# One vector operation in place of two in the router and the selection, and each gather of the first group behind the matrix that used to come after it

## The chip, the cores and the metric

The kernel runs on one core of a Trainium2 chip. The metric is the device time of one execution in microseconds (us). The engines meant below are PE (TensorE, the matrix engine), DVE (VectorE), ACT (ScalarE), POOL (GpSimd) and SP (SyncE, which here only issues transfers from main memory).

## What is computed

One layer of an encoder on 256 tokens of width 2048: attention, and behind it a mixture of 32 experts. The change touches only the second half, which in the reference is (cut):

```python
def hierarchical_moe(h, rg_w, rg_b, re_w, re_b, w_gu, w_d):
    g_prob = jax.nn.softmax((hf @ rg_w).astype(f32) + rg_b.astype(f32), axis=-1)
    g_p, g_idx = lax.top_k(g_prob, 1)
    e_logits = ((hf @ re_w).astype(f32) + re_b.astype(f32)).reshape(n_tok, MOE_GROUPS, MOE_EXPERTS_PER_GROUP)
    e_logits = e_logits[jnp.arange(n_tok), g_idx[:, 0]]
    e_p, e_idx = lax.top_k(jax.nn.softmax(e_logits, axis=-1), MOE_TOP_K)
    e_p = e_p / jnp.sum(e_p, axis=-1, keepdims=True)
    weight = g_p * e_p
    expert_id = g_idx * MOE_EXPERTS_PER_GROUP + e_idx
    ...
        g, u = jnp.split(xb @ w_gu[e], 2, axis=-1)
        return (jax.nn.silu(g) * u) @ w_d[e]
```

Each token chooses one of 4 groups and in it 2 of 8 experts. An expert has a matrix `w_gu` of 2048 x 1024 and a matrix `w_d` of 512 x 2048, all in float32, together 12 MB. The 32 experts make 400 MB, which must all be read.

## The kernel before

Attention comes first; its weights and those of the experts go through one **ring** of six slots of 2 MB in the on-chip memory (`ring`). SP issues the loads in a fixed order (`load_item`), one per slot; ahead of each it waits until the semaphore `w_used` says that PE has read what lay in the slot. An expert takes six loads (four quarters of `w_gu`, j = 0 to 3, and two halves of `w_d`, j = 4 and 5). Five of them of the first two experts lie in other tiles that were free early (`SPARE`, `HALF_SPARE`: the tiles `arena`, `ada_ring`, `region_a`, `held`), so they need no slot.

Experts are worked on in **groups of four** (`moe_group`, 8 groups: the first is written out, the next six are a loop on each engine, the last is written out as the tail). Further groups for experts with over 32 tokens are planned by `plan_further_items`; none ran in the profile. In a group:

- DVE makes the selection `sel_w`, 128 tokens x (4 experts x 32 slots) for each of the two token halves (`for a in range(TT)`, TT = 2), as a comparison of a rank table with slot numbers, and from it `sel`, scaled by the norm of the token. With that it raises `sel_ready`.
- PE gathers the tokens of the four experts by matmuls with `sel`, in four parts of the width: `gather(0)` to `gather(3)`, each 8 matmuls of 128 x 128 into a PSUM bank of its own.
- For each part DVE reads the bank, scales and shifts it into `x_items` (two operations of 128 x 512) and raises `items_ready`.
- For each expert i PE multiplies `x_items` by the four quarters of `w_gu`. For i = 0 quarter j needs part j of `x_items`, so it waits for `items_ready`, j + 1. Before the change the gathers run one ahead: gather 0, gather 1, quarter 0, gather 2, quarter 1, gather 3, quarter 2, quarter 3. After each of the quarters `w_used` rises by one.
- While PE does quarter 3 of the first expert, DVE in the first group runs `weigh` (the weights of the chosen experts, small operations) and then scales `sel_w` by them (`selw_ready`); PE transposes that.
- ACT and DVE form `silu(g) * u` (`gate_exp`, `hid_ready`), PE transposes it and multiplies by the two halves of `w_d`.
- After four experts PE adds the results to the tokens (`y_done`, `y_added`), and the next group begins.

In the first group DVE also runs `plan_further_items` behind the third expert's results, over 40 small operations. SP waits for its end (`tables_ready`) before it issues the loads of the second group's first expert.

**Ahead of the first group** stands the router. DVE turns the logits of both token halves into a choice (`first_max` for the group, then `by_group` and `e_log`, the logits of the chosen group; `first_max` twice more for the two experts; `outer`, which spreads the choice over 32 experts into `chosen`). PE ranks the tokens by a few small matmuls, and DVE makes `rank1`, from which the selection is made. Every operation of DVE here waits for the one before it (`step.link`). PE has nothing else to do until `sel_ready`.

Of the kernel before, what the change touches and what calls it, by code (L numbers as in the profile page):

```python
# [17 lines left out]
P = 128  # L18
T = 256
TT = T // P  # L20
# [4 lines left out]
EXPERTS, GROUPS, PER_GROUP = 32, 4, 8  # L25
FF = 512
FT = FF // P
SLOTS = 32
QUAD = 4
# [38 lines left out]
def encoder_layer(nc, x, c, ada_w, ada_b, norm1_g, norm2_g, router_g_w, router_g_b, router_e_w, router_e_b,  # L68
# [3 lines left out]
    ALU, ACT, AX = mybir.AluOpType, mybir.ActivationFunctionType, mybir.AxisListType  # L72
    X = AX.X

    ctx = ExitStack()
    with ctx:
# [25 lines left out]
        slot_no = sb("slot_no", [P, SLOTS])  # L102
# [50 lines left out]
        sel = carve(4096, TT, QUAD, SLOTS)  # L153
        sel_w = carve(4352, TT, QUAD, SLOTS)
# [4 lines left out]
        rank1 = carve(6016, TT, ITEMS)  # L159
        weight = carve(6112, TT, ITEMS)  # L160
        rt = carve(6208, 448)
        logits = rt[:, 0:72].rearrange("p (a n) -> p a n", a=TT)
        by_group = rt[:, 72:136].rearrange("p (a n) -> p a n", a=TT * GROUPS)
# [43 lines left out]
        ssq, rstd = stat[:, 0:2], stat[:, 2:4]  # L207
# [392 lines left out]
        def _(pe):  # L600
# [444 lines left out]
            def moe_group(g, first=False, tail=False):  # L1045
# [78 lines left out]
                for i in range(2 if tail else QUAD):  # L1124
                    m = g * QUAD + i
                    for j in range(4):
# [3 lines left out]
                        if i == 0 and j < 3:  # L1130
                            gather(j + 1)
# [19 lines left out]
                        if j < 3:  # L1151
                            last.then_inc(w_used, 1)
                    last.then_inc(w_used, 1)
# [332 lines left out]
        def _(dve):  # L1486
# [344 lines left out]
            for a in range(TT):  # L1831
                part = by_group[:, GROUPS * a:GROUPS * (a + 1), :]
                step.link(v.tensor_tensor(part, logits[:, a, GROUPS:].rearrange("p (g e) -> p g e", g=GROUPS),
                                          g_hot[:, a, :].unsqueeze(2).to_broadcast([P, GROUPS, PER_GROUP]),
                                          ALU.mult))
                step.link(v.reduce_sum(e_log[:, a, :], part.rearrange("p g e -> p e g"), X))
# [8 lines left out]
            def outer(dst, per_expert):  # L1845
                for a in range(TT):
                    ins = v.tensor_tensor(dst[:, a, :].rearrange("p (g e) -> p g e", g=GROUPS),
                                          g_hot[:, a, :].unsqueeze(2).to_broadcast([P, GROUPS, PER_GROUP]),
                                          per_expert[:, a:a + 1, :].to_broadcast([P, GROUPS, PER_GROUP]), ALU.mult)
                    if a < TT - 1:  # L1850
                        step.link(ins)
                return ins
# [69 lines left out]
            def moe_group(g, tab, first_group=False, tail=False):  # L1922

                wide4 = [P, QUAD, SLOTS]
                for a in range(TT):
                    r = rank1[:, a, bass.ds(tab * QUAD, QUAD)]
                    step.link(v.tensor_tensor(sel_w[:, a, :, :], slot_no[:].unsqueeze(1).to_broadcast(wide4),
                                              r.unsqueeze(2).to_broadcast(wide4), ALU.is_equal))

                for a in range(TT):  # L1930
                    ins = v.tensor_scalar(sel[:, a, :, :], sel_w[:, a, :, :], rstd[:, a:a + 1], None, ALU.mult)  # L1931
                    if a < TT - 1:
                        step.link(ins)
                ins.then_inc(sel_ready, 1)
# [13 lines left out]
                for a in range(TT):  # L1948
                    w = weight[:, a, bass.ds(tab * QUAD, QUAD)]
                    ins = v.tensor_tensor(sel_w[:, a, :, :], sel_w[:, a, :, :], w.unsqueeze(2).to_broadcast(wide4),  # L1950
                                          ALU.mult)
                    if a < TT - 1:
                        step.link(ins)
                ins.then_inc(selw_ready, 1)
# [70 lines left out]
            per_group = TT + (TT - 1) + 4 + (TT - 1) + 3 * QUAD  # L2025
# [51 lines left out]
```

## Time and profile before

| | |
|---|---|
| median of 3 runs | 1489.13 us (1489.03 to 1489.66) |
| profiled execution, its time | 1489.31 us |
| its span in the trace | 1487.5 us |
| PE busy | 1148.3 us, 77% |
| DVE busy | 633.7 us, 43% |
| read from main memory | 575.02 MB, 388 GB/s over the span |

The span is what the trace covers; 1.8 us of the execution's own time lie around it. The shares of busy time are averages over two very different stages: attention and its weights up to some 550 us, and the experts behind it.

### The profile page before, as it was taken

To read this page: it belongs to the slowest core of one execution; us is meant where nothing else is said; L and a number is where in the kernel's file an instruction comes from. 1 tells how busy PE (TensorE), PEld (TensorE's weight loads), DVE (VectorE), ACT (ScalarE), POOL (GpSimd) and SP (SyncE) were. 2 spreads that over 40 slices of the span, in tenths; PEclk is the share of its full clock that TensorE was granted. 3 is DMA by queue.
4 is the path that set the end of the run, shared out by engine and by line. 5 is a ranking of instruction groups with operands and counts; after the bars stand their busy time and mean duration, and the time that the engine had idled before them with its cause. 6 is when DMAs were issued, how large, how long until landed. Compare 5 with 4: busy or idle time off the path is not lost.

```text
span 1487.5 us, 20513 instructions
## 1 busy us (share of the span) xinstructions
PE 1148.3 (77%) x8480; PEld 736.7 (50%) x8480; DVE 633.7 (43%) x1026; ACT 175.3 (12%) x395; POOL 95.7 (6%) x122
## 2 busy tenths in 40 slices
PE   3899999999999998767567667668558558567655
PEld 3788888888888885333133124224214224224222
DVE  4766768777747524452132123124114114214214
ACT  3011242222134120300000000000000000000002
POOL 3211101121100000000000000000000000000001
PEclk9999999999999999979789689789779879879888
DMA  8999999999995477999999999999999999999996
GB/s 316 383 387 388 399 376 383 385 392 381 357 374 195 165 299 304 425 420 404 428 427 429 428 430 428 427 429 429 428 429 428 428 429 428 428 428 429 427 427 244
DMA packets 116139, 577.92 MB, mean 389 GB/s; under 512 B 10250, under 2 KB 51296, under 8 KB 90484
## 3 DMA queue, kind: packets, MB, share of 16 engines
q1 hardware_dynamic: 89572, 474.37, 78.4%
q0 software_dynamic: 26512, 102.77, 17.9%
q8 instruction: 40, 0.66, 0.2%
q14 instruction: 15, 0.12, 0.0%
HBM read 575.02 MB, written 2.10 MB: 388 GB/s over the span
## 4 chain that ended last, share of the span: by engine, by line
PE 53%; DMA 37%; DVE 6%; issue 1%; ACT 1%; SPq 0%; DVEq 0%; ACTq 0%
DMA ring<-in_moe_w_gu_dram 26%; PE psum L770 9%; PE psum L1147 8%; PE psum L734 7%; DMA ring<-in_moe_w_d_dram 7%; PE psum L1054 5%; PE psum L1176 4%; PE psum L744 4%; DMA ring<-in_da_w_in_dram 4%; PE psum L1199 3%; PE psum L965 3%; PE psum L886 2%; PE psum L878 2%; DVE arena L1525 1%; PE psum L681 1%
## 5 line engine op out<-in xcount | busy, mean ns | idle before, releaser
L1147 PE MATMUL psum<-ring,ada_ring 128*32 128x256 f32 x3696 | 276.7, 450 | 143.5 <-DMA ring<-in_moe_w_gu_dram 143.4
L1147 PEld LDWEIGHTS psum<-ring,ada_ring 128*32 128x32 f32 x3696 | 125.0, 121 | 290.3 <-DMA ring<-in_moe_w_gu_dram 190.3
L1176 PE MATMUL psum<-ring,arena 128*32 128x512 f32 x960 | 157.0, 803 | 27.0 <-ACT arena L1444 16.0
L1975 DVE TENSOR_SCALAR arena<-arena 128x128 f32<-128x128 f32 x32 | 7.3, 227 | 348.5 <-ACT arena L1438 348.5
L1992 DVE TENSOR_TENSOR arena<-psum,arena 32x512 f32<-32x512 f32 x108 | 74.1, 686 | 187.5 <-PE psum L1176 177.3
L770 PE MATMUL psum<-region_b,ring 128*128 128x256 f32 x512 | 113.8, 380 | 4.1 <-ACT region_b L1301 2.6
L734 PE MATMUL psum<-region_b,ring 128*128 128x256 f32 x512 | 112.0, 379 | 0.0
L770 PEld LDWEIGHTS psum<-region_b,ring 128*128 128x128 f32 x512 | 96.6, 190 | 18.0 <-ACT region_b L1301 3.3
L734 PEld LDWEIGHTS psum<-region_b,ring 128*128 128x128 f32 x512 | 96.7, 190 | 12.8
L1438 ACT ACTIVATE arena<-psum 128x128 f32<-128x128 f32 x32 | 8.9, 278 | 783.9 <-PE psum L1147 742.2
L1176 PEld LDWEIGHTS psum<-ring,arena 128*32 128x32 f32 x960 | 37.2, 134 | 124.9 <-issue 83.0
L1525 DVE SCALAR_TENSOR_TENSOR arena<-ada_ring,silu_c,arena 128x512 f32<-128x512 f32 x120 | 90.2, 752 | 19.1 <-DMA ada_ring<-in_ada_w_dram 15.4
L1054 PE MATMUL psum<-arena,region_b 128*128 128x128 f32 x512 | 74.8, 311 | 22.6 <-DVE arena L1931 17.5
L1054 PEld LDWEIGHTS psum<-arena,region_b 128*128 128x128 f32 x512 | 70.2, 222 | 35.4 <-issue 34.1
L1545 DVE SCALAR_TENSOR_TENSOR held<-ada_ring,silu_c,held 128x1024 f32<-128x1024 f32 x60 | 77.1, 1284 | 15.2 <-DMA ada_ring<-in_ada_w_dram 13.5
L1545 DVE SCALAR_TENSOR_TENSOR arena<-ada_ring,silu_c,arena 128x1024 f32<-128x1024 f32 x60 | 77.0, 1283 | 9.4 <-DMA ada_ring<-in_ada_w_dram 7.8
L770 PE MATMUL psum<-ring,region_b 128*128 128x256 f32 x256 | 58.7, 386 | 5.5 <-DMA ring<-in_da_w_in_dram 5.5
L594 POOL TENSOR_TENSOR region_b<-region_a,ada_ring 128x1024 f32<-128x1024 f32 x3 | 7.1, 2357 | 864.1 <-DVE region_a L1968 864.1
L1165 PE MATMUL psum<-ident,arena 128*128 128x128 f32 x30 | 10.6, 353 | 66.1 <-DVE arena L1978 66.1
L567 POOL DMA_DIRECT2D ada_ring<-in_ada_w_dram x64 | 45.1, 704 | 234.0 <-DVE held L1545 108.6
L1199 PE MATMUL psum<-arena 128*128 128x512 f32 x112 | 51.6, 615 | 8.7 <-DVE arena L1992 4.8
L744 PE MATMUL psum<-ring,region_b 128*128 128x256 f32 x256 | 55.9, 379 | 0.0
(269 smaller groups left out, 1112.1 us busy)
## 6 DMA issues: line engine op xcount, KB each, us to landing
ring<-in_moe_w_gu_dram SPq DMA_DIRECT2D x123, 2048.0 KB, 25.6
ring<-in_moe_w_d_dram SPq DMA_DIRECT2D x62, 2048.0 KB, 24.4
ada_ring<-in_ada_w_dram POOLq DMA_DIRECT2D x88, 1024.0 KB, 10.9
ring<-in_da_w_in_dram SPq DMA_DIRECT2D x15, 2048.0 KB, 34.7
ring<-in_da_w_in_dram SPq DMA_DIRECT2D x18, 1024.0 KB, 23.8
ring<-in_da_w_out_dram SPq DMA_DIRECT2D x8, 2048.0 KB, 20.6
ada_ring<-in_ada_w_dram POOLq DMA_DIRECT2D x16, 512.0 KB, 12.9
ring<-in_moe_w_d_dram SPq DMA_DIRECT2D x8, 512.0 KB, 19.4
```

The source lines that it names most:

```text
L567: gp.dma_start(ada_ring[:, j % ADA_CH, :].rearrange("p (k n) -> p k n", k=2), w_ada[:, 2 * j:2 * j + 2, bass.ds(n * 2 * ADA_BLK, 2 * ADA_B ...
L734: last = mm(psum[:, B_Q + j, T * i:T * (i + 1)], slot16(s)[:, k, P * i:P * (i + 1)], h_t[:, k, :], start=k == 0, stop=k == KT - 1)
L744: last = mm(psum[:, B_V, VD * a:VD * (a + 1)], h_t[:, k, P * a:P * (a + 1)], slot16(s)[:, k, :], start=k == 0, stop=k == KT - 1)
L770: return mm(psum[:, bank, T * a:T * (a + 1)], lhs, rhs, **flags)
L965: last = mm(psum[:, bank, 0:VD], lhs[:, k, :], w[:, k0 + k, :], start=k == 0 and not more, stop=k == 7, skip_group_check=True)
L1054: last = mm(psum[:, B_G + q, P * kk:P * (kk + 1)], x_res[:, a, P * k:P * (k + 1)], sel[:, a, :, :].rearrange("p a b -> p (a b)"), start=a ...
L1147: last = mm(psum[32 * n:32 * n + 32, B_GU, 0:256].rearrange("p (a b) -> p a b", a=2), x_items[:, k, SLOTS * i:SLOTS * (i + 1)], w[:, :, n ...
L1176: last = mm(psum[32 * n:32 * n + 32, B_D + i % 2, :], hid_t[:, k, :], w[:, kk, n, :], start=k == 0, stop=k == FT - 1)
L1199: mm(psum[:, B_G + n, :], sel_t[:, a, :], o_items[:, 512 * n:512 * (n + 1)], start=True, stop=True).then_inc(y_done, 1)
L1525: ins = v.scalar_tensor_tensor(out=acc_b, in0=w, scalar=silu_c[:, k:k + 1], in1=acc_b, op0=ALU.mult, op1=ALU.add)
L1545: ins = v.scalar_tensor_tensor(out=row, in0=w, scalar=silu_c[:, k:k + 1], in1=row, op0=ALU.mult, op1=ALU.add)
L1992: v.tensor_tensor(o, src, gate2[32 * n:32 * n + 32, cols], ALU.mult).then_inc(o_ready, 1)
```

## The change

Two kinds of edit. First, on DVE, pairs of operations, one for each token half, become single operations over both: the product and the sum that make `e_log`, the two calls of `outer`, and in every group the comparison for `sel_w`, its scaling into `sel` (a tensor_scalar with a column becomes a tensor_tensor with a broadcast column) and its scaling by the weights. Second, on PE, in the first group only, `gather(j + 1)` no longer stands ahead of quarter j of the first expert but behind it.

```diff
-                        if i == 0 and j < 3:
+                        if i == 0 and j < 3 and not first:
                             gather(j + 1)
                         if spare is not None:
                             pe.wait_ge(spare_loaded[spare], 32)
...
                         if j < 3:
                             last.then_inc(w_used, 1)
+                        if first and i == 0 and j < 3:
+                            gather(j + 1)
...
-            for a in range(TT):
-                part = by_group[:, GROUPS * a:GROUPS * (a + 1), :]
-                step.link(v.tensor_tensor(part, logits[:, a, GROUPS:].rearrange("p (g e) -> p g e", g=GROUPS),
-                                          g_hot[:, a, :].unsqueeze(2).to_broadcast([P, GROUPS, PER_GROUP]),
-                                          ALU.mult))
-                step.link(v.reduce_sum(e_log[:, a, :], part.rearrange("p g e -> p e g"), X))
+            both = [P, TT, GROUPS, PER_GROUP]
+            hot_groups = g_hot.unsqueeze(3).to_broadcast(both)
+            step.link(v.tensor_tensor(by_group, logits[:, :, GROUPS:].rearrange("p a (g e) -> p a g e", g=GROUPS),
+                                      hot_groups, ALU.mult))
+            step.link(v.reduce_sum(e_log, by_group.rearrange("p a g e -> p a e g"), X))
...
             def outer(dst, per_expert):
-                for a in range(TT):
-                    ins = v.tensor_tensor(dst[:, a, :].rearrange("p (g e) -> p g e", g=GROUPS),
-                                          g_hot[:, a, :].unsqueeze(2).to_broadcast([P, GROUPS, PER_GROUP]),
-                                          per_expert[:, a:a + 1, :].to_broadcast([P, GROUPS, PER_GROUP]), ALU.mult)
-                    if a < TT - 1:
-                        step.link(ins)
-                return ins
+                return v.tensor_tensor(dst.rearrange("p a (g e) -> p a g e", g=GROUPS), hot_groups,
+                                       per_expert.unsqueeze(2).to_broadcast(both), ALU.mult)
...
-                wide4 = [P, QUAD, SLOTS]
-                for a in range(TT):
-                    r = rank1[:, a, bass.ds(tab * QUAD, QUAD)]
-                    step.link(v.tensor_tensor(sel_w[:, a, :, :], slot_no[:].unsqueeze(1).to_broadcast(wide4),
-                                              r.unsqueeze(2).to_broadcast(wide4), ALU.is_equal))
-
-                for a in range(TT):
-                    ins = v.tensor_scalar(sel[:, a, :, :], sel_w[:, a, :, :], rstd[:, a:a + 1], None, ALU.mult)
-                    if a < TT - 1:
-                        step.link(ins)
-                ins.then_inc(sel_ready, 1)
+                both4 = [P, TT, QUAD, SLOTS]
+                r = rank1[:, :, bass.ds(tab * QUAD, QUAD)]
+                step.link(v.tensor_tensor(sel_w, slot_no[:].unsqueeze(1).unsqueeze(1).to_broadcast(both4),
+                                          r.unsqueeze(3).to_broadcast(both4), ALU.is_equal))
+                v.tensor_tensor(sel, sel_w, rstd.unsqueeze(2).unsqueeze(3).to_broadcast(both4), ALU.mult)\
+                    .then_inc(sel_ready, 1)
```

What stands in a row on PE at the head of the first group, before the change (L1054 is a gather, L1147 a quarter of `w_gu`, L1043 the last matmul of the ranks, L1159 the transposes of `sel_w`; the trace counts each float32 matmul twice, so x8 here is x16 there):

```order
L1043 MATMUL psum<-arena,ones 128x32
L1054 MATMUL psum<-arena,region_b 128x128 x16
L1147 MATMUL psum<-ring,ada_ring 32x256 x16
L1054 MATMUL psum<-arena,region_b 128x128 x8
L1147 MATMUL psum<-ring,ada_ring 32x256 x16
L1054 MATMUL psum<-arena,region_b 128x128 x8
L1147 MATMUL psum<-ring,ada_ring 32x256 x16
L1147 MATMUL psum<-arena,ada_ring 32x256 x8
L1147 MATMUL psum<-ada_ring 32x256 x8
L1159 MATMUL psum<-ident,arena 128x128 x2
```

And after it, at the same place (the transposes are L1161 here):

```order
L1043 MATMUL psum<-arena,ones 128x32
L1054 MATMUL psum<-arena,region_b 128x128 x8
L1147 MATMUL psum<-ring,ada_ring 32x256 x16
L1054 MATMUL psum<-arena,region_b 128x128 x8
L1147 MATMUL psum<-ring,ada_ring 32x256 x16
L1054 MATMUL psum<-arena,region_b 128x128 x8
L1147 MATMUL psum<-ring,ada_ring 32x256 x16
L1054 MATMUL psum<-arena,region_b 128x128 x8
L1147 MATMUL psum<-arena,ada_ring 32x256 x8
L1147 MATMUL psum<-ada_ring 32x256 x8
L1161 MATMUL psum<-ident,arena 128x128 x2
```

The same matmuls stand there; the second gather has moved from ahead of the first quarter to behind it, the third and the fourth likewise by one quarter, so that each quarter now stands directly behind the gather whose result it needs.

On DVE, from the end of the router to the first parts of `x_items`, before the change (L1847 is `outer`, L1856 `rank1`, L1927 the comparison, L1931 the scaling into `sel`, L1940 and L1943 `x_items`):

```order
L1843 TENSOR_TENSOR arena<-arena 128x16
L1847 TENSOR_TENSOR arena<-arena 128x32 x2
L1856 SCALAR_TENSOR_TENSOR arena<-psum,arena 128x2x32
L1927 TENSOR_TENSOR arena<-slot_no,arena 128x128 x2
L1931 TENSOR_SCALAR arena<-arena,stat 128x128 x2
L1940 TENSOR_TENSOR ada_ring<-psum,a 128x512
L1943 TENSOR_TENSOR ada_ring<-ada_ring,mod 128x512
```

And after it (the comparison is L1922, the scaling L1924, `x_items` L1931 and L1934):

```order
L1844 TENSOR_TENSOR arena<-arena 128x16
L1847 TENSOR_TENSOR arena<-arena 128x64
L1852 SCALAR_TENSOR_TENSOR arena<-psum,arena 128x2x32
L1922 TENSOR_TENSOR arena<-slot_no,arena 128x256
L1924 TENSOR_TENSOR arena<-arena,stat 128x256
L1931 TENSOR_TENSOR ada_ring<-psum,a 128x512
L1934 TENSOR_TENSOR ada_ring<-ada_ring,mod 128x512
```

Three pairs of operations have become three operations of twice the size; nothing has changed its place.

## Rows read from the trace of the kernel before

**Rows 1.** Stretches: bounds, length, busy of PE, PEld, DVE, ACT, POOL, clock, DMA, GB/s

```profile
560.00:568.00 8.00, 7.29 (x64) 6.18 (x64) 3.35 (x7) 0.00 (x0) 0.00 (x0) 0.79 0.08 32
...
588.00:670.00 82.00, 59.21 (x547) 27.68 (x543) 41.95 (x89) 15.43 (x15) 7.23 (x2) 0.88 1.00 423
670.00:674.00 4.00, 4.00 (x56) 2.83 (x52) 1.44 (x3) 0.00 (x0) 0.00 (x0) 1.00 0.73 225
674.00:780.00 106.00, 70.27 (x650) 30.23 (x639) 27.06 (x51) 2.61 (x9) 0.00 (x0) 0.84 1.01 427
...
1400.00:1463.00 63.00, 36.98 (x379) 13.63 (x383) 9.38 (x19) 3.15 (x8) 0.00 (x0) 0.81 1.01 422
```

**Rows 2.** Timeline of SP's queue: start us, length, the load issued

```profile
568.19 0.33 SPq L477 DMA_DIRECT2D ring<-in_moe_w_d_dram  x1
...
670.74 0.33 SPq L474 DMA_DIRECT2D ring<-in_moe_w_gu_dram  x1
```

**Rows 3.** Timeline of PE, head of the first group (gathers L1054, quarters L1147)

```profile
560.71 5.47 PE L1054 MATMUL psum<-arena,region_b 128*128 128x128 f32 x32 [1.17 <-DVE arena L1931]
566.10 2.02 PE L1147 MATMUL psum<-ring,ada_ring 128*32 128x256 f32 x32
568.05 2.05 PE L1054 MATMUL psum<-arena,region_b 128*128 128x128 f32 x16
570.03 2.02 PE L1147 MATMUL psum<-ring,ada_ring 128*32 128x256 f32 x32
...
576.71 1.11 PE L1147 MATMUL psum<-ada_ring 128*32 128x256 f32 x16
```

**Rows 4.** Timeline of DVE there: the parts of x_items

```profile
564.43 0.69 DVE L1940 TENSOR_TENSOR ada_ring<-psum,a 128x512 f32<-128x512 f32 x1 [3.78 <-PE psum L1054]
565.16 0.69 DVE L1943 TENSOR_TENSOR ada_ring<-ada_ring,mod 128x512 f32<-128x512 f32 x1
...
570.14 0.69 DVE L1940 TENSOR_TENSOR ada_ring<-psum,a 128x512 f32<-128x512 f32 x1 [2.51 <-PE psum L1054]
```

**Rows 5.** Timeline of DVE, router to selection, and an operation of 256 columns

```profile
548.95 0.42 DVE L1799 TENSOR_TENSOR arena<-psum,ada_ring 128x256 f32<-128x256 f32 x1 [6.25 <-PE psum L878]
...
554.27 0.18 DVE L1833 TENSOR_TENSOR arena<-arena 128x32 f32<-128x32 f32 x1
...
555.20 0.17 DVE L1820 TENSOR_REDUCE arena<-arena 128x2 f32<-128x16 f32 x1
...
557.76 0.42 DVE L1847 TENSOR_TENSOR arena<-arena 128x32 f32<-128x32 f32 x2
...
559.39 0.62 DVE L1927 TENSOR_TENSOR arena<-slot_no,arena 128x128 f32<-128x128 f32 x2
560.04 0.61 DVE L1931 TENSOR_SCALAR arena<-arena,stat 128x128 f32<-128x128 f32 x2
```

**Rows 6.** Timeline at the first expert's end: weigh, selection, gate

```profile
575.40 0.18 DVE L1863 COPY arena<-psum 128x32 f32<-128x32 f32 x1
...
577.90 0.62 DVE L1950 TENSOR_TENSOR arena<-arena 128x128 f32<-128x128 f32 x2
577.91 0.28 ACT L1438 ACTIVATE arena<-psum 128x128 f32<-128x128 f32 x1 [20.02 <-PE psum L1147]
578.43 0.22 DVE L1975 TENSOR_SCALAR arena<-arena 128x128 f32<-128x128 f32 x1
```

**Rows 7.** Timeline from the plan to the second group's first gathers

```profile
637.58 0.23 DVE L1975 TENSOR_SCALAR arena<-arena 128x128 f32<-128x128 f32 x1
...
662.99 5.60 PE L1054 MATMUL psum<-arena,region_b 128*128 128x128 f32 x32 [5.13 <-issue]
```

**Rows 8.** Busy time by stretches, for the clock (columns as in rows 1)

```profile
561.00:564.00 3.00, 3.00 (x16) 3.00 (x16) 0.00 (x0) 0.00 (x0) 0.00 (x0) 0.50 0.00 0
581.50:584.50 3.00, 3.00 (x20) 0.85 (x16) 0.00 (x0) 0.00 (x0) 0.00 (x0) 0.50 1.03 434
594.00:597.00 3.00, 0.70 (x5) 0.29 (x9) 1.76 (x4) 0.70 (x2) 0.00 (x0) 1.00 1.01 415
```

More of the change, by code:

```diff
@@ L162, in encoder_layer @@
         logits = rt[:, 0:72].rearrange("p (a n) -> p a n", a=TT)
-        by_group = rt[:, 72:136].rearrange("p (a n) -> p a n", a=TT * GROUPS)
+        by_group = rt[:, 72:136].rearrange("p (a g n) -> p a g n", a=TT, g=GROUPS)
         chosen = rt[:, 136:200].rearrange("p (a n) -> p a n", a=TT)
@@ L1947, in moe_group @@
                     weigh()
[L1948 to L1954, printed above, removed]
+                w = weight[:, :, bass.ds(tab * QUAD, QUAD)]
+                v.tensor_tensor(sel_w, sel_w, w.unsqueeze(3).to_broadcast(both4), ALU.mult).then_inc(selw_ready, 1)
                 def keep_last(q):
@@ L2024, in _ @@
             moe_group(0, 0, first_group=True)
-            per_group = TT + (TT - 1) + 4 + (TT - 1) + 3 * QUAD
+            per_group = 1 + 4 + 3 * QUAD
             extra_groups = dve.value_load(extra_i[0:1, EXTRA:EXTRA + 1], min_val=0, max_val=EXTRA // QUAD)
```

## The prediction

> **What bounds the kernel now.** I read the stretches first, since the share of busy time is a mean over stages. From 674 us to 1463 us the DMA engines are busy all the time and move 422 to 429 GB/s [rows 1]. In that stretch the experts' matrices come as fast as they can, and PE and DVE wait for them. Nothing that either engine does faster or slower there can move the end; what counts is the moment at which the stream starts to run without a hole. So I looked for holes. There is a large one from 560 to 568 us (share 0.08, 32 GB/s), then a full stretch from 588 to 670 us (423 GB/s), and a last one from 670 to 674 us (share 0.73, 225 GB/s: against 428 GB/s, (1 - 225/428) x 4 = 1.9 us of transfer are missing) [rows 1].
>
> The last hole is the one that dates the stream. It ends with a load that SP issues at 670.74 us [rows 2], as PE has just read the first quarter of the second group's first expert: the gathers began at 662.99 us [rows 7], and the slot was free at 670.7. The ring had run dry a moment before. What comes before 662.99 is a chain without a DMA wait in it: back over the fourth expert of the first group, whose gate DVE took up at 637.58, right at the end of its plan for further groups [rows 7], over the third and the second expert to the first one [rows 6], to the gathers [rows 3], to the selection and the router [rows 5]. So a microsecond more or less in that chain moves the load at 670.74 us by as much, and with it the end. For a longer chain this is exact, since the hole is already there; a shorter one would gain until the hole of about 2 us is closed.
>
> **The gathers.** Before the change PE has no wait from 566.10 us on: quarter, gather, quarter, gather, quarter, quarter, the last ending at 576.71 + 1.11 = 577.82, so 11.72 us [rows 3]. DVE makes a part of `x_items` in two operations, 0.73 us from one start to the next and 0.69 us for the second, 1.42 us in all [rows 4], and all of it lies under the gather or quarter that PE does meanwhile. After the change each quarter stands right behind its own gather, and PE has nothing else to do while DVE works. That cover is gone, and the 1.42 us come in full. One round is then:
>
> - gather, 568.05 to 570.03: 1.98 us [rows 3];
> - from its end to DVE's start, 570.03 to 570.14: 0.11 us [rows 3, 4];
> - DVE: 1.42 us [rows 4];
> - from DVE's end to PE's start, as between the selection (560.04 + 0.61) and the first gather (560.71): 0.06 us [rows 3, 5];
> - quarter, 566.10 to 568.05: 1.95 us [rows 3].
>
> That makes 5.52 us. From the start of quarter 0 to the end of quarter 3 it takes 1.95 + 3 x 5.52, and 0.07 for the end of the last quarter (2.02 long instead of its step of 1.95): 18.58 us. Against 11.72 that is **+6.86 us**. The second gather, which now stands inside, is in that figure; ahead of quarter 0 it leaves almost nothing, because quarter 0 had to wait for `x_items` anyway: these were ready at 565.16 + 0.69 = 565.85 [rows 4], with the 0.06 above 565.91, and it began at 566.10. **-0.19 us**. This is all that the new order saves ahead of the first freed slot. The second slot comes 5.52 us after the first and no longer 568.05 to 572.0, 3.9 us; the third later still.
>
> **DVE ahead of the gathers.** Every operation waits for the one before, and PE waits for the last. The four small operations for `e_log` take 554.27 to 555.20, 0.93 us, about 0.23 each [rows 5]. What a wider one costs I take from 128 columns at about 0.31 against 256 at 0.42 us [rows 5]: 0.11 for 128 columns, so 0.03 for 32 more. Two operations of 0.26 make 0.52: -0.41. `outer`: 0.42 for two, one of 0.20 + 0.03: -0.19. Comparison and scaling: from 559.39 to 560.65, 1.26 us for four [rows 5]; two of 0.42 with a gap of 0.04: 0.88, -0.38. The scaling becomes a tensor_tensor with two broadcast inner dimensions, a form the trace does not show. Its bounds are one half's 0.31 below and two halves' 0.62 above; I take 0.42, since the comparison (a tensor_tensor with broadcast) and the scaling cost the same for 128 columns, 0.62 and 0.61 for two [rows 5]. For all five edits the same bounds give 0 to about 1.3 us of saving; I take the sum, **-0.98 us**.
>
> **The weights and the gate of the first expert.** `weigh` and the scaling of `sel_w` run from 575.40 to the gate's first operation at 578.43, 3.03 us [rows 6]. They lose 0.19 (`outer`) and 0.20 (0.62 to 0.42). Counted from 575.40, quarter 3 used to end at +2.42 and the gate came 0.61 behind it. Now `x_items`, whose last operation ends 0.08 behind that point, starts quarter 3 after 0.06, and it ends at +0.08 + 0.06 + 2.02 = +2.16; DVE would reach the gate at 3.03 - 0.39 = +2.64, 0.48 behind it. ACT would let it at 0.42 (0.09 to its start, 0.28, 0.05), so DVE stays last. **-0.13 us**.
>
> **Every other group.** The selection's saving of some 0.4 us lies where the stream is full. In the second group, the one ahead of the last hole, PE's idle time ahead of the gathers is ended by "issue", its own way into the loop, not by DVE [rows 7]. 0 us for all of them, and nothing moves in the tail.
>
> **The sum** is 6.86 - 0.19 - 0.98 - 0.13 = +5.56 us. Against the profiled execution's own 1489.31 us (span 1487.5) this gives 1494.9; that execution is 0.2 us above the median, so I forecast **1494.7 us**. Cover elsewhere? The loads for the third and fourth expert are issued as slots come free, the first that matters behind the first expert, so they are late by the same 5.5 us, and so is the plan behind which the fourth expert waits.
>
> **The clock.** PE's granted clock was at 0.50 (1.2 GHz) from 561 to 564 us, just as the first gathers ran, and again from 581.5 to 584.5; ahead of the first, DVE had let PE wait 1.17 us for the selection [rows 3, 8]. At 594 to 597 it had 0.70 us of work in 3 us and the clock stayed at 1.00 [rows 8]. Each such stretch costs 3 x (1 - 0.5) = 1.5 us when matmuls fill it. After the change PE is busy 3.93 of 5.52 us in each round, far more than in these pauses. So I count no new fall and leave the two old ones where they are. If both happened to miss the work, the end would come at 1494.7 - 3.0 = 1491.7; falls do not keep still from run to run, so this is the low side of my range, and a larger price of DVE's wider forms the other way adds up to 1.0.
>
> **Rivals.**
>
> *The clock falls between the rounds.* Three pauses of 1.59 us now stand where PE had none. For it: two of the idle spells in this stage were followed by half clock. Against it: a spell with a quarter of the work was not [rows 8]. One fall costs 1.5 us, two 3.0: 1496.2 or 1497.7 us. The Trainium skill, "TensorE: Matmul & The Clock Gate", section "A second HAM failure mode: psum-queue depth-cycling", speaks for this rival: short idle moments between groups of matmuls, as the engine goes from PSUM bank to bank, are enough to make the clock swing between its two levels. By that rule the time would be that of two falls, by the rows on the pauses that of none.
>
> *The first hole dates the stream, and the change gains.* Then the load at 568.19 us [rows 2] is what counts. It would come 0.19 + 0.98 = 1.2 us earlier, and the end at 1487.9 us. For it: DMA does nothing from 560 to 568, and a slot freed early is worth a transfer. Against it: the stream still has a hole at 670 us. It decides only if the ring is still full at 670.74 us, which needs more than the missing 1.9 us of slack.
>
> *The extra wait is hidden.* If something else than DVE held the fourth expert (its `w_gu`, for one), the chain could lengthen without a price. The time would be that of before, 1489.1 us, to 1490. Against it: DVE goes from its plan into the gate at once at 637.58 [rows 7].
>
> **Chances.** The forecast with its own spread (1491.7 to 1496) 0.70; the clock rival 0.14; the gain by the first hole 0.06; hidden 0.07; a hole elsewhere that I don't see 0.03. The range, 1491.3 to 1497.7, leaves the two rivals without a loss outside, and what lies beyond two falls. A measurement of this kernel can tell from no change about 0.2%, 3 us. Faster than 1486.1: 0.03; within: 0.10; slower than 1492.1: 0.87 (the forecast's share below 1492.1 is small).
>
> **What would show it.** The gathers of the first group in four rows of about 2 us, each followed by a quarter, with PE idle 1.5 to 1.6 us ahead of each quarter, ended by DVE's second `x_items` operation. The first load of the stage issued near 567 us, the next 5.5 us later. The gate of the first expert at 578.4 + 5.5 = 584; the load after the last hole at 676.3; the full stretch behind it as long as before. DVE from `e_log` to `sel_ready` 1.0 us shorter. The forecast is wrong if the load at 670.74 moves by 5.5 and the end does not, or if the clock in the rounds is 0.50.

## The result, and the profile after

The changed kernel took 1496.80 us (median of 6, 1495.32 to 1498.34) against 1489.17 us before (median of 6, 1488.93 to 1489.66): a ratio of 1.0047, interval 1.0035 to 1.0059. It is slower, by 7.0 us by the ratio and 7.6 by the medians. The same two kernels were timed twice more beside the experiments, on chips whose executions spread more: 1.0037 (1.0024 to 1.0051) and 1.0036 (1.0024 to 1.0049), so +5.5 and +5.4 us by the ratios. The three intervals (5.2 to 8.8 us, 3.6 to 7.6, 3.6 to 7.3) overlap, so these timings do not tell 7.0 us from 5.5. One execution of the experiment with a fill (4834.68 us, while its others lie under 1498) is left out of every figure below. The profiled execution of the changed kernel took 1498.34 us, the slowest of its six, with a span of 1496.5 us: 9.0 us more span than before.

Timeline of PE in the changed kernel, head of the first group (gathers L1054, quarters L1147):

```profile
559.68 2.73 PE L1054 MATMUL psum<-arena,region_b 128*128 128x128 f32 x16 [0.79 <-DVE arena L1924]
564.09 3.64 PE L1147 MATMUL psum<-ring,ada_ring 128*32 128x256 f32 x32 [1.67 <-DVE ada_ring L1934]
567.66 2.05 PE L1054 MATMUL psum<-arena,region_b 128*128 128x128 f32 x16
571.31 2.03 PE L1147 MATMUL psum<-ring,ada_ring 128*32 128x256 f32 x32 [1.60 <-DVE ada_ring L1934]
573.28 2.05 PE L1054 MATMUL psum<-arena,region_b 128*128 128x128 f32 x16
576.93 2.04 PE L1147 MATMUL psum<-ring,ada_ring 128*32 128x256 f32 x32 [1.60 <-DVE ada_ring L1934]
...
583.46 1.12 PE L1147 MATMUL psum<-ada_ring 128*32 128x256 f32 x16
587.55 5.34 PE L1178 MATMUL psum<-ring,arena 128*32 128x512 f32 x32 [0.37 <-ACT arena L1446]
```

This answers to [rows 3]. The pauses are there, 1.60 us each, and each is ended by DVE's second `x_items` operation (L1934). The round is 5.62 us long (571.31 to 576.93). Quarter 0 took 3.64 and not 2.0 us. From the first gather to the end of quarter 3 it is 584.58 - 559.68 = 24.90 us, for 577.82 - 560.71 = 17.11 before, where the clock was low over the gathers too [rows 8].

Timeline of SP's queue in the changed kernel, to set beside [rows 2]:

```profile
567.78 0.33 SPq L477 DMA_DIRECT2D ring<-in_moe_w_d_dram  x1
573.40 0.33 SPq L477 DMA_DIRECT2D ring<-in_moe_w_d_dram  x1
579.02 0.33 SPq L474 DMA_DIRECT2D ring<-in_moe_w_gu_dram  x1
590.68 0.33 SPq L474 DMA_DIRECT2D ring<-in_moe_w_gu_dram  x1
...
677.57 0.33 SPq L474 DMA_DIRECT2D ring<-in_moe_w_gu_dram  x1
```

The first slot is free 0.41 us earlier than before, all the others later, and the load that ends the last hole comes 6.83 us later. Stretches of the changed kernel (columns as in [rows 1]):

```profile
561.00:564.00 3.00, 1.42 (x7) 1.12 (x6) 1.38 (x2) 0.00 (x0) 0.00 (x0) 0.50 0.00 0
564.00:567.50 3.50, 3.42 (x32) 1.58 (x32) 0.00 (x0) 0.00 (x0) 0.00 (x0) 0.50 0.02 5
...
586.50:591.00 4.50, 3.77 (x21) 1.08 (x25) 0.29 (x1) 0.28 (x1) 0.00 (x0) 0.69 0.01 4
...
620.00:670.00 50.00, 31.38 (x219) 11.40 (x219) 31.53 (x70) 3.22 (x7) 0.00 (x0) 0.90 1.00 424
...
676.00:684.00 8.00, 8.00 (x107) 5.64 (x100) 2.91 (x5) 0.00 (x0) 0.00 (x0) 1.00 0.88 330
...
690.00:780.00 90.00, 58.48 (x531) 22.08 (x531) 20.39 (x35) 1.66 (x6) 0.00 (x0) 0.83 1.01 428
...
1400.00:1470.00 70.00, 40.62 (x403) 14.32 (x395) 8.69 (x17) 3.15 (x8) 0.00 (x0) 0.78 1.01 423
```

Three things are to be seen. The clock stood at 0.50 from 561 to 567.5 us, over gather 0 and quarter 0. It fell during gather 0, ahead of the first pause of the rounds, just where it fell before the change, and came back some 3 us later than there; no fall began in one of the pauses. From 586.5 to 591 the DMA engines did nothing, a hole that the kernel before did not have. And from 690 us on the stream is as full as it was. Two places further on: PE's wait for the second half of the fourth expert's `w_d`, and the selection of the second group (timeline of several engines):

```profile
650.96 1.92 PE L1178 MATMUL psum<-ring,arena 128*32 128x512 f32 x16 [0.88 <-DMA ring<-in_moe_w_d_dram]
...
667.88 0.42 DVE L1922 TENSOR_TENSOR arena<-slot_no,arena 128x256 f32<-128x256 f32 x1 [1.64 <-issue]
668.34 0.42 DVE L1924 TENSOR_TENSOR arena<-arena,stat 128x256 f32<-128x256 f32 x1
...
669.97 1.33 PE L1054 MATMUL psum<-arena,region_b 128*128 128x128 f32 x5 [4.58 <-issue]
```

The end itself. In both kernels PE waits for the same last load and then has a fixed row of work; first the kernel before, then the changed one, timeline of PE:

```profile
1465.10 1.65 PE L1101 MATMUL psum<-ring,held 128*32 128x128 f32 x32 [1.63 <-DMA ring<-in_moe_w_d_dram]
1466.68 3.05 PE L1111 MATMUL psum<-arena 128*128 128x512 f32 x4
```

```profile
1472.84 1.93 PE L1101 MATMUL psum<-ring,held 128*32 128x128 f32 x32 [1.63 <-DMA ring<-in_moe_w_d_dram]
1474.70 3.78 PE L1111 MATMUL psum<-arena 128*128 128x512 f32 x4
```

The stream's last load arrived 7.74 us later. From there to the end of the span it is 22.4 us before and 23.7 after; in several experiments it is 20.7, with the same two matmul groups at 1.08 and 1.98 us instead. So 1.3 us of the 9.0 came from how long the clock was low in the tail of these two executions. The other 7.7 are the 6.83 of the last hole, and 0.9 between that load and the last one, which the changed kernel does not always pay (see the size, below).

### The profile page after: what moved, and what is told of

Read it like the earlier page. It is cut to its first block, busy times and chain, and to the rows that moved or that the text cites. A ratio compares the mean times of both kernels' runs of the same rounds, so it can differ in the third digit from the quotient of the medians.

```text
span 1496.5 us, 20452 instructions
## 1 busy us (share of the span) xinstructions
PE 1150.6 (77%) x8480; PEld 732.7 (49%) x8480; DVE 629.3 (42%) x998; ACT 175.1 (12%) x395; POOL 95.5 (6%) x122
## 4 chain that ended last, share of the span: by engine, by line
PE 53%; DMA 40%; DVE 4%; issue 1%; ACT 1%; SPq 0%; DVEq 0%; ACTq 0%
DMA ring<-in_moe_w_gu_dram 25%; DMA ring<-in_moe_w_d_dram 10%; PE psum L770 9%; PE psum L1147 8%; PE psum L734 7%; PE psum L1054 5%; PE psum L1178 4%; PE psum L744 4%; DMA ring<-in_da_w_in_dram 4%; PE psum L1201 3%; PE psum L965 3%; PE psum L886 2%; PE psum L878 2%; PE psum L681 1%; PE psum L706 1%
## 5 line engine op out<-in xcount | busy, mean ns | idle before, releaser
L1147 PE MATMUL psum<-ring,ada_ring 128*32 128x256 f32 x3696 | 280.8, 455 | 155.7 <-DMA ring<-in_moe_w_gu_dram 150.8
L1147 PEld LDWEIGHTS psum<-ring,ada_ring 128*32 128x32 f32 x3696 | 125.2, 123 | 305.3 <-DMA ring<-in_moe_w_gu_dram 198.6
L1054 PE MATMUL psum<-arena,region_b 128*128 128x128 f32 x512 | 69.3, 296 | 18.2 <-DVE arena L1924 13.7
L1054 PEld LDWEIGHTS psum<-arena,region_b 128*128 128x128 f32 x512 | 64.5, 206 | 31.9 <-issue 31.0
```

The costliest lines, as they stand in the source:

```text
L1054: last = mm(psum[:, B_G + q, P * kk:P * (kk + 1)], x_res[:, a, P * k:P * (k + 1)], sel[:, a, :, :].rearrange("p a b -> p (a b)"), start=a ...
L1147: last = mm(psum[32 * n:32 * n + 32, B_GU, 0:256].rearrange("p (a b) -> p a b", a=2), x_items[:, k, SLOTS * i:SLOTS * (i + 1)], w[:, :, n ...
```

## The experiments

All ratios are against the kernel before on the same chip in the same call, with the 95% interval. A date below is a start in the profile. Each run has one profile, and the clock falls at other places in each, so dates far behind the rounds can differ by over 2 us between profiles of the same kernel.

**The two kinds of edit apart.** The new order alone, on DVE's operations as before:

```diff
-                        if i == 0 and j < 3:
+                        if i == 0 and j < 3 and not first:
                             gather(j + 1)
...
+                        if first and i == 0 and j < 3:
+                            gather(j + 1)
```

> Only the new order of the gathers, DVE as before. Theory A (the chain of the first group dates the stream, and the pauses add to it): 6.86 - 0.19 = +6.7 us by the working of the prediction, and up to 1.6 more where a quarter runs at half clock, so 1495.8 to 1497.4. Rival B (the two edits hurt together, for instance because the earlier selection shifts the gathers into a half clock): clearly under the +7.6 of the whole change, near +5.5, 1494.7.

Measured: 1497.31 us against 1490.19, 1.0049 (1.0036 to 1.0061), +7.1 us by the medians, +7.3 by the ratio. No quarter ran at half clock in its profile, and still it took 22.58 us from the first gather to the end of quarter 3 (562.64 to 585.22). Rival B's +5.5 lies just inside the interval (5.4 to 9.1 us), so this timing alone does not exclude it. The two runs that follow do: DVE's part alone makes the kernel faster, so it adds nothing to the loss. The order is the whole loss.

DVE's wider operations alone (all edits of the diff but those to `gather`):

> Only DVE's wider operations, gathers in the old order. Theory A: the chain ahead of the gathers shorter by 1.06 (as measured in the changed kernel: gathers at 559.68 for 560.71, of which 0.06 are from before the router), the gate 0.2 to 0.4 earlier, and the second group's selection 0.5 shorter, so -1.2 to -1.9 us: 1487.3 to 1487.9. Rival (all of it is cover that the stream hides): 1489.2. Rival B: slower than before.

Measured: 1487.70 us against 1490.19, 0.9986 (0.9977 to 0.9994): a gain of 2.1 us by the ratio, 2.5 by the medians. Once more, on another chip:

> DVE's wider operations alone, once more: -1.5 to -2.5 if the first result (-2.5) holds; within 0.5 of the kernel before if it was the chips' spread.

Measured: 1488.46 us against 1490.06, 0.9989 (0.9979 to 0.9999), -1.6 us. So DVE's part is a gain of about 2 us, with intervals that reach from 0.1 to 3.4. Its profile is also the clean picture of the old order, since the clock did not fall there (timeline of PE, first run of the two):

```profile
559.21 3.84 PE L1054 MATMUL psum<-arena,region_b 128*128 128x128 f32 x32 [0.79 <-DVE arena L1922]
562.97 2.02 PE L1147 MATMUL psum<-ring,ada_ring 128*32 128x256 f32 x32
...
573.58 1.08 PE L1147 MATMUL psum<-ada_ring 128*32 128x256 f32 x16
```

First gather to end of quarter 3: 574.66 - 559.21 = 15.45 us. The kernel before had 17.11, the difference of 1.66 being the half clock of [rows 8]. This very profile lost its lead again behind the gathers: its first two experts' `w_d` matmuls took 5.34 and 6.49 us where 3.64 is the time at full clock. Its last load reached PE only 0.12 us earlier than before (1464.98), that of the second profile 0.58 us (1464.52). The gain is shown by the timings; the profiles do not show by which way it comes to the end.

**The size.** The changed kernel again:

> The changed kernel once more, beside the three others on one chip. Theory A with additive parts: the new order alone gave +7.1 and DVE's part alone -2.5 against the kernel before on their chip, so +4.6 to +5.6. Rival C (a quarter at half clock belongs to the pair of edits, and the ring runs dry a second time): +7.6 again.

Measured: 1495.87 us against 1490.34, 1.0037 (1.0024 to 1.0051), +5.5 us (3.6 to 7.6). Rival C's +7.6 is at the very edge of that. The ring did run dry a second time (no transfer from 584 to 588 us), but no quarter was slow. Its timeline of PE shows the rounds without a fall of the clock:

```profile
559.55 2.05 PE L1054 MATMUL psum<-arena,region_b 128*128 128x128 f32 x16 [0.79 <-DVE arena L1924]
563.27 2.04 PE L1147 MATMUL psum<-ring,ada_ring 128*32 128x256 f32 x32 [1.67 <-DVE ada_ring L1934]
565.24 2.05 PE L1054 MATMUL psum<-arena,region_b 128*128 128x128 f32 x16
568.89 2.04 PE L1147 MATMUL psum<-ring,ada_ring 128*32 128x256 f32 x32 [1.60 <-DVE ada_ring L1934]
...
581.05 1.12 PE L1147 MATMUL psum<-ada_ring 128*32 128x256 f32 x16
```

582.17 - 559.55 = 22.62 us, against 15.45 in the old order: **+7.17 us** at full clock. A third time:

> The changed kernel on the chip of this call, for the size: 5.5 if the forecast's sum is the typical one and the first timing (+7.6) had more of the clock's falls, 7.6 if the repeat (+5.5) was the odd one.

Measured: 1494.60 us against 1490.06, 1.0036 (1.0024 to 1.0049). By the ratio +5.4 us, by the medians +4.5; the same stretch took 22.59 us (559.60 to 582.19). The +7.6 of the first timing did not come back, though the intervals overlap.

How far one profile can be trusted shows when those of the same kernel are set side by side (us):

| profile | quarter 3 ends | gate of the fourth expert | load that ends the last hole | last load reaches PE | time of the execution |
|---|---|---|---|---|---|
| before | 577.82 | 637.58 | 670.74 | 1465.10 | 1489.31 |
| changed, first | 584.58 | 644.12 | 677.57 | 1472.84 | 1498.34 |
| changed, second | 582.17 | 641.63 | 674.63 | 1469.61 | 1493.78 |
| changed, third | 582.19 | 643.29 | 677.19 | 1471.53 | 1494.15 |
| DVE alone, first | 574.66 | 637.24 | 670.88 | 1464.98 | 1487.55 |
| DVE alone, second | 576.67 | 636.16 | 669.09 | 1464.52 | 1488.46 |

The second and the third profile of the changed kernel agree at quarter 3 and are 2.56 us apart at the last hole. Of these, 1.70 are the third expert's `w_d` matmuls, 3.64 us in the one (618.37) and 5.34 in the other (618.31). From the load of the last hole to the last load it takes 795.3, 795.0 and 794.3 us in the three, 794.4 before.

**Is it DVE's time that is exposed?** In both kernels, in the first group only, `x_items` is made by one operation; the shift is left out of the computation there:

```diff
-                    step.link(v.tensor_tensor(x_items[:, ks, :],
+                    product = v.tensor_tensor(x_items[:, ks, :],
...
+                    if first_group:
+                        product.then_inc(items_ready, 1)
+                        continue
+                    step.link(product)
```

> The changed kernel, but in the first group x_items is made by one DVE operation instead of two (the shift is left out of the computation there). If DVE's time is exposed once per round, each of the four waits shrinks by 0.73: -2.9 us against the changed kernel. Rival (the pauses do not count, the ring's slots do): within 0.5 of the changed kernel.

Measured: 1492.51 us against 1490.34, 1.0011 (1.0001 to 1.0022); against the changed kernel on the same chip (1495.87, 1.0037) -3.4 us by the medians, and the two intervals do not touch. The rounds shrank as they should (timeline of PE):

```profile
562.68 2.03 PE L1147 MATMUL psum<-ring,ada_ring 128*32 128x256 f32 x32 [0.94 <-DVE ada_ring L1931]
564.64 2.05 PE L1054 MATMUL psum<-arena,region_b 128*128 128x128 f32 x16
567.57 2.03 PE L1147 MATMUL psum<-ring,ada_ring 128*32 128x256 f32 x32 [0.88 <-DVE ada_ring L1931]
```

A round is 4.89 us, 0.73 less, and the pauses 0.88.

> The same cut in the kernel before (the shift is left out in the first group). There DVE's time lies under gathers and quarters: 0 to -0.2 us against the kernel before, 1489.0 to 1489.2 on the first chip. Rival (DVE's x_items limit both orders): -2.9.

Measured: 1489.68 us, 0.9992 (0.9983 to 1.0000), -0.7 us by the medians and -1.2 by the ratio (0 to 2.5), which leaves the rival's 2.9 outside, and from the first gather to the end of quarter 3 exactly the 17.11 us of before (560.30 to 577.41). The same 0.69 us operation, four times, is worth 3.4 us in the one order and about 1 us or nothing in the other: that is the cover the new order gave up.

**Order against slots.** Only the second gather moved behind quarter 0:

```diff
-                        if i == 0 and j < 3:
+                        if i == 0 and j < 3 and not (first and j == 0):
...
+                        if first and i == 0 and j == 0:
+                            gather(1)
```

> Kernel before with only the second gather moved behind quarter 0; the others run one ahead as before, so PE has one pause less its cover: quarter 0 starts 0.19 earlier and the second gather's 1.98 us come behind it. Theory A: +1.8 us, 1491.0, if the clock keeps its fall where it is, and up to 1.6 more if quarter 0 takes the half clock that the second gather had. Rival (moving one gather is free): 1489.2.

Measured: 1491.30 us against 1490.19, 1.0005 (0.9996 to 1.0014), +0.7 us by the ratio. Between the two expectations and not told apart from either by the timing. In its profile the stretch took 580.27 - 560.72 = 19.55 us for 17.11, with the clock low over gather 0 and quarter 0. The last load reached PE 1.8 us later than before (1466.92), but this does not confirm the expected 1.8: the load that ends the last hole came only 0.62 us later (671.36), since the first expert's `w_d` matmuls ran at full clock here (3.64 us for 5.34).

All four gathers ahead of quarter 0:

```diff
                 gather(0)
+                if first:
+                    for q in range(1, 4):
+                        gather(q)
```

> Kernel before with all four gathers of the first group ahead of quarter 0. PE has the same work and no pause, quarter 3 ends at the same time, but the first ring slot comes free 3.9 us later and the second 2 us later. Theory A: the end stays, 1489.2 (within 0.5). Rival (the first hole dates the stream): +3.9, 1493.1.

Measured: 1491.80 us against 1490.19, 1.0005 (0.9995 to 1.0015): +0.8 by the ratio (-0.7 to 2.2), +1.6 by the medians. That excludes the rival's 3.9 and does not tell the result from my 0. The profile has a trace of the rival all the same. Its first gather happened to start at 563.00, but the clock did not fall, and quarter 3 ended at 577.87, as before. The fourth expert's gate came on time too (637.70 for 637.58), though a lead of 1.85 us from the first expert's `w_d` matmuls, which ran at full clock here, was lost by then, in part by a wait of 1.31 us for a half of the third expert's `w_d` (615.64). Then the timeline of PE has

```profile
645.01 3.31 PE L1179 MATMUL psum<-ring,arena 128*32 128x512 f32 x16 [1.72 <-DMA ring<-in_moe_w_d_dram]
652.20 10.04 PE L1202 MATMUL psum<-arena 128*128 128x512 f32 x16 [3.87 <-DVE arena L2013]
```

where the kernel before had no wait:

```profile
640.33 4.86 PE L1176 MATMUL psum<-ring,arena 128*32 128x512 f32 x32 [0.37 <-ACT arena L1444]
649.06 8.80 PE L1199 MATMUL psum<-arena 128*128 128x512 f32 x16 [3.87 <-DVE arena L2010]
```

The load after the last hole is issued at 675.36, 4.62 us later than before. Against the kernel before, only the 1.72 us of the wait come from the ring's loads, restarted at 572.45 for 568.19; the rest is clock behind it (the second half of `w_d` 3.31 us where 1.92 is the time at full clock, the adding 10.04 for 8.80, the next gathers 5.97 for 5.60). So the first slot's date has a cover that ends: in this profile 4.26 us of lateness became a wait of 1.72, so it is 2.5 us at most, and the timing, at most 2.2 us for slots that are 3.9 later, asks for 1.7 at least. Some 2 us, then, as an estimate; what lies beyond costs, as the rival "the first hole dates the stream" has it.

**The same lateness without the order.** The kernel before with work that nobody reads on PE behind quarter 3 of the first expert, so that the first four slots come free as before:

```diff
+                    if first and i == 0:
+                        for _ in range(17):
+                            mm(psum[:, B_D, 0:T], ident[:], x_res[:, 0, 0:T], start=True, stop=True)
```

> The kernel before, with 17 matmuls that nobody reads (256 columns, 0.456 us each, 7.75 us) on PE behind the first expert's quarter 3, at full clock. The first four ring slots come free exactly as before, and only the chain behind is late, by about 6.6 us (PE was to wait till 580.3 anyhow, and two transposes with ACT's copy come behind the block). Theory A (lateness of the chain is all that counts, wherever it arises): +6.6, the price of the new order. Rival (the new order costs by the later slots, the chain has cover): well under +3.

Measured: 1494.50 us against 1490.06, 1.0033 (1.0020 to 1.0045), +4.9 us by the ratio. The block took 7.61 us, and the stretches show the same hole that the changed kernel has:

```profile
584.00:590.00 6.00, 5.07 (x37) 2.74 (x39) 0.00 (x0) 0.66 (x2) 0.00 (x0) 1.00 0.26 109
```

The rival (slots make the price, the chain has cover) falls. Lateness of the chain costs wherever it arises. The 6.6 expected is still inside the interval (3.0 to 6.7 us). In the profile the `w_d` matmuls behind the block begin 6.55 us later than before (587.58 for 581.03) and end 4.85 later, since they ran at full clock here (3.64 us for 5.34); the fourth expert's gate is then 4.85 us later too (642.43 for 637.58). So the chain carries its lateness on without loss. That the block kept the clock up is not shown: those matmuls took 3.64 us without it as well, in the profiles of the shortened `x_items` in the old order, of the four gathers first and of the one moved gather.

**The clock.** The changed kernel with PE kept busy in the pauses:

```diff
-        KEEP_WARM = 10
+        KEEP_WARM = 11
...
+            mm(psum[:, B_GU, 0:T], ident[:], x_res[:, 0, 0:T], start=True, stop=True)
...
+                def keep_busy():
+                    for _ in range(3):
+                        mm(psum[:, B_D, 0:T], ident[:], x_res[:, 0, 0:T], start=True, stop=True)
```

with `keep_busy()` behind each gather of the first group.

> The changed kernel with matmuls that nobody reads (three of 256 columns, 1.37 us at full clock) in each of the four pauses, one more ahead of the ranks and one behind them, so that PE is never idle for long in the rounds. If half clock on quarter 0 is a part of the excess over the forecast, the quarter takes 2.0 and not 3.6 us and the end comes 1.6 earlier than the changed kernel's. If the clock has no part, the same or up to 0.5 later. If the fill itself runs at half clock, it takes 2.7 us and delays quarter 0 by 1.1.

Measured: 1496.16 us (median of six) against 1490.34, 1.0040 (1.0026 to 1.0055), the changed kernel beside it 1.0037. In the profile the fill fits and no quarter is slow:

```profile
564.09 1.46 PE L1126 MATMUL psum<-region_b,ident 128*128 128x256 f32 x6
565.92 2.02 PE L1154 MATMUL psum<-ring,ada_ring 128*32 128x256 f32 x32 [0.37 <-DVE ada_ring L1942]
```

The stretch took 22.54 us (562.20 to 584.74), as long as without the fill where the clock had not fallen (22.62). So a fall in the rounds is not what makes the change slow as a rule. In the first profile it cost 24.90 - 22.62 = 2.28 us, but the kernel before had paid 1.66 at the same place in its own profile, so only 0.6 us of the difference between these two come from it. Of four profiles of the new order without a fill and with unshortened rounds (the first, the two repeats, the order alone) one had it.

**A better version.** DVE's part in the old order, with the same two matmuls around the ranks and no fill:

> DVE's wider operations in the old order, and two more matmuls that nobody reads, one ahead of the ranks and one behind them, so that PE is not idle ahead of the first gather. If that keeps the clock up in the first two gathers, 1.5 us are saved in the executions where it fell: -3 to -4 against the kernel before. If the clock falls elsewhere instead, or if the slots' loads set the rest of the stage, no more than DVE's part alone.

Measured: 1489.27 us against 1490.06, 0.9992 (0.9983 to 1.0001). No better than DVE's part alone (0.9989 beside it). The clock stayed up over the gathers (3.84 us for both) and was low over the first expert's `w_d` matmuls, 5.34 us. But both profiles of DVE's part without the two matmuls have these same two figures, so the matmuls are not shown to have done anything. The best version here is DVE's part alone; by the timings it is not told apart from this one.

## Why the prediction was right

The forecast was +5.56 us, 1494.7 us, in a range of 1491.3 to 1497.7. The first timing gave 1496.8, inside the range and 2 us above the forecast; the two repeats gave ratios that mean +5.5 and +5.4 us. By its own steps:

- **What bounds.** The last hole moved with the chain of the first group and the full stretch behind it stayed full, as said. The best evidence is the block of useless work: it made the kernel slower by 4.9 us without touching the order, and in its profile `w_d`'s end, the fourth gate and the load after the hole are 4.85, 4.85 and 5.05 us later. That the first profile has 6.76 at quarter 3 and 6.83 at the hole is less than it seems: the two repeats have 4.35 and 3.89, and 4.37 and 6.45, as the clock falls on the way. I had called the dates of the first slots free of charge; they have a cover of only some 2 us (four gathers first).
- **The gathers, +6.86.** At full clock, by the difference of the clean profiles, 18.90 us from quarter 0 to the end of quarter 3 against 11.69: +7.21. The round was 5.62 us, not 5.52: PE began 0.15 us after DVE's end (576.09 + 0.69 to 576.93), where I had taken 0.06 from the selection. The shortened `x_items` showed the mechanism in both directions.
- **Quarter 0 earlier, -0.19.** Mis-sized: -0.04 (3.72 for 3.76 us behind the first gather). I had read it from [rows 3] at half clock, where the gathers took 5.4 us and not 3.8.
- **DVE ahead of the gathers, -0.98.** The gathers began at 559.68 for 560.71, of which 0.07 had arisen ahead of the edits (`e_log`'s first operation at 554.20 for 554.27): -0.96. The scaling as a tensor_tensor with two broadcast dimensions, the form without a row, took 0.42 to 0.43 us, the value taken and not one of the bounds.
- **The gate, -0.13.** It came at 584.96, 0.38 us behind the end of quarter 3, before 0.61: -0.23.
- **The second group, 0.** Nearly so. DVE's selection there got 0.52 us shorter (660.36 to 661.76 before, 667.88 to 668.76 after), and I had held that PE's idle time ahead of the gathers does not depend on it. The idle times (timelines of PE, the shortened `x_items` in the old order, the one moved gather, and the new selection with the two matmuls) are:

```profile
662.25 6.11 PE L1054 MATMUL psum<-arena,region_b 128*128 128x128 f32 x32 [4.57 <-DVE arena L1931]
663.33 5.83 PE L1054 MATMUL psum<-arena,region_b 128*128 128x128 f32 x32 [4.66 <-DVE arena L1933]
662.60 5.72 PE L1055 MATMUL psum<-arena,region_b 128*128 128x128 f32 x32 [4.92 <-issue]
```

  Over all fourteen profiles the idle time is 4.57 to 5.13 us with the old selection (mean of six 4.91) and 4.58 to 4.92 with the new one (mean of eight 4.73). PE began between 0.69 and 1.54 us after DVE's end. So about 0.2 of the 0.52 us came through; the least idle time is the same with either. What sets it stays open.
- **The sum, with what was measured**, is 7.21 - 0.04 - 0.96 - 0.23 - 0.2 = +5.8 us, with both kernels at full clock over the first gathers. The forecast's mechanism is confirmed; that it agrees with the ratios of the repeats to 0.1 us is luck, since a timing is good to about 2 us here, the errors of the terms partly cancelled, and the profile before had 1.66 us of half clock in the gathers that the repeats' profiles had not.
- **What the forecast left out** shows in the first profile: 0.6 us more for the clock's fall over the first gather and quarter 0 than its fall had cost before; a second hole in the stream at 586.5 to 591, since the loads behind it wait for the first expert's end while the ring runs dry; 0.88 us that PE later waited for a half of `w_d`; 0.9 us between the last hole and the last load; and 1.3 us in the tail. The second hole is in the repeats as well (no transfer from 584 to 587 us), but the second profile has no wait for `w_d` behind it, so its price is not shown. I had not seen it.

On the **rivals**: the clock was at 0.50 in the first profile over quarter 0, which I had named as a sign that the forecast is wrong, but it had fallen during gather 0, at 561 us, as before the change, and no profile of the new order has a fall that began in a pause of the rounds. The Trainium skill's rule, "TensorE: Matmul & The Clock Gate", section "A second HAM failure mode: psum-queue depth-cycling", would have made falls between the rounds the typical case; the rounds of the two repeats and of the order alone ran at full clock with pauses of 1.60 us, so here the rows on the pauses decide, not the rule. The first-hole rival had a true core, a cover of some 2 us that the forecast took for endless. That the wait is hidden fell with the first result.

**Open** remains how the 2 us between the first timing and the repeats divide between the clock and the chips. There is one profile for each set of timings, falls of the clock stand at different places in them, and the intervals overlap. Open too is what makes the way from the last hole's load to the last load 794.1 to 794.4 us in half of the profiles and 795.0 to 795.6 in the other half. It is not the change: the changed kernel has both (794.3 and 795.3), and so has the old order with DVE's wider operations (794.1 and 795.4).

## What to carry to other kernels

A product that waits for its own operand's post-processing wants another piece of work between the two; "one ahead" is not a habit but the cover of 1.6 us each time, and whoever gives up this cover to free buffers earlier frees only the first one earlier (here by 0.05 us, counted from the first gather: 565.35 - 559.55 for 565.06 - 559.21) and all the others later. Where a full transfer stream bounds the kernel, find its last hole and cost every edit by what it does to the chain ahead of that hole: there time lost counted in full (the block of useless work); that it counts for nothing behind the hole was taken for granted and not tested. Before a wait is put down to another engine at a fixed distance, look at more than two profiles: behind DVE's selection, PE began 1.23 us later before the change and 1.21 after it, which looks like a rule, and between 0.69 and 1.54 in the others.

## What the runs showed of the hardware that was not expected

- One operation over 256 columns took 0.42 us where two of 128 took 0.62 to 0.65 with the step between, and one over 64 columns 0.22 where two of 32 took 0.42: the second half of a pair cost 0.02 to 0.13 us. The forecast had taken these sizes; what no row had shown is that the form with two broadcast dimensions costs no more (0.42 to 0.43 us for 256 columns).
- Where the clock falls changes from profile to profile, and each fall shows in the work that it meets: the first expert's `w_d` matmuls took 5.34 us in six of the fourteen profiles and 3.64 in five; the first two gathers of the old order took 5.47 us in two profiles and 3.84 in four. Two added matmuls around the ranks, or a block of 7.61 us, are not shown to have moved a fall.
